# Start of a four-layer decoder trunk: order of the first loads, and the banks of the first norm's transposes

## The reference

```python
h = x
h = h + _even_mixer(_rmsnorm(h, norm_mix_even), ...)     # layer 0
...
def _rmsnorm(x, g):
    y = x * rsqrt(mean(x * x, axis=-1) + 1e-6)
    return y * g

def _even_mixer(h, ...):
    proj = h @ w_in                                       # 256 x 1024 @ 1024 x 2560
    qa, ka, va, ub, vb = split(proj, [512, 1024, 1536, 2048])
    qa, ka = rope(qa), rope(ka)                           # then differential attention
    lam = exp(sum(lam_q1 * lam_k1)) - exp(sum(lam_q2 * lam_k2)) + lam_init
    vb = layernorm(gelu(vb), sgu_ln_g, sgu_ln_b)
    ws = where(causal, sgu_w, 0)                          # 4 groups of 128 x 128
    mixed = einsum('gpq,bnqgc->bnpgc', ws, vb) + sgu_b
...
```

## Time and profile before

| | |
|---|---|
| median of 3 runs | 1367.97 us (1367.27 to 1369.31) |
| the profiled execution's own time | 1367.54 us |
| its span | 1365.8 us |
| TensorE matmul busy | 1344.9 us, 98% of the span |
| VectorE busy | 1129.7 us, 83% |
| ScalarE busy | 1006.0 us, 74% |
| granted TensorE clock, mean | 0.998 |

### The profile page before, as it was taken

The page is one execution under the profiler, slowest core; times in us unless marked ns, Lnnn a source line. Parts: engine busy times, 40 slices in busy tenths (PEclk is TensorE's granted clock), DMA queues, the critical chain, the costliest instruction groups (busy, mean ns, idle before and its releaser), DMA issues.

```text
span 1365.8 us, 19316 instructions
## 1 busy us (share of the span) xinstructions
PE 1344.9 (98%) x6874; PEld 1137.8 (83%) x6874; DVE 1129.7 (83%) x1153; ACT 1006.0 (74%) x1184; POOL 93.4 (7%) x117
## 2 busy tenths in 40 slices
PE   8999999999999999999999999999999999999997
PEld 7779989988788888888888888888888888888885
DVE  5675655566569999998999999999999999999996
ACT  6664544457558878788878888887888888788775
POOL 2201000000038600000000000000000000000010
PEclk9999999999999999999999999999999999999999
DMA  9457854354589999999999999999999999999960
GB/s 329 174 201 272 313 186 155 125 184 148 183 299 381 388 394 397 396 391 370 387 384 370 378 394 377 371 391 378 376 368 393 371 379 388 383 369 383 391 248 33
DMA packets 180621, 436.96 MB, mean 320 GB/s; under 512 B 4070, under 2 KB 8332, under 8 KB 180572
## 3 DMA queue, kind: packets, MB, share of 16 engines
q1 hardware_dynamic: 176816, 422.74, 83.7%
q0 software_dynamic: 3680, 13.54, 2.7%
q10 hardware_dynamic: 76, 0.02, 0.0%
HBM read 423.18 MB, written 13.11 MB: 319 GB/s over the span
## 4 chain that ended last, share of the span: by engine, by line
PE 94%; DVE 2%; ACT 2%; issue 1%; DMA 0%; ACTq 0%; SPq 0%; DVEq 0%
PE ps L1615 27%; PE ps L1617 26%; PE ps L1616 26%; PE ps L1870 3%; PE ps L1871 3%; PE ps L1872 3%; PE ps L2148 2%; ACT w_hi L660 1%; DVE w_lo L1062 1%; PE ps L1673 1%; PE ps L1642 0%; PE ps L2116 0%; ACT e L715 0%; PE ps L1625 0%; DMA h<-in_x 0%
## 5 line engine op out<-in xcount | busy, mean ns | idle before, releaser
L1491 DVE TENSOR_TENSOR w_lo<-ring_a,w_hi 128x1024 fp32r<-128x1024 f32 x384 | 459.1, 1223 | 36.7 <-ACT w_hi L939 18.3
L939 ACT ACTIVATE w_hi<-ring_a 128x1024 fp32r<-128x1024 f32 x384 | 399.0, 1057 | 61.6 <-PE ps L1617 61.5
L1491 DVE TENSOR_TENSOR w_lo<-ring_b,w_hi 128x1024 fp32r<-128x1024 f32 x288 | 344.5, 1223 | 22.8 <-ACT w_hi L939 8.0
L1615 PE MATMUL ps<-w_hi,xg_hi 128*128 128x512 f32 x896 | 354.2, 395 | 0.1
L1617 PE MATMUL ps<-w_hi,xg_lo 128*128 128x512 f32 x896 | 349.2, 390 | 0.0
L1616 PE MATMUL ps<-w_lo,xg_hi 128*128 128x512 f32 x896 | 348.7, 389 | 0.0
L939 ACT ACTIVATE w_hi<-ring_b 128x1024 fp32r<-128x1024 f32 x288 | 300.7, 1059 | 50.3 <-PE ps L1617 50.3
L1062 DVE TENSOR_TENSOR w_lo<-ring_a,w_hi 128x1024 fp32r<-128x1024 f32 (+2 forms) x119 | 141.5, 1199 | 107.7 <-ACT w_hi L660 107.6
L660 ACT ACTIVATE w_hi<-ring_a 128x1024 fp32r<-128x1024 f32 (+2 forms) x119 | 121.7, 1032 | 125.7 <-PE ps L1872 63.7
L1615 PEld LDWEIGHTS ps<-w_hi,xg_hi 128*128 128x128 f32 x896 | 168.3, 188 | 35.9 <-DVE w_lo L1491 3.1
L1617 PEld LDWEIGHTS ps<-w_hi,xg_lo 128*128 128x128 f32 x896 | 168.1, 188 | 35.8
(11 more groups left out here) (333 smaller groups left out, 1388.1 us busy)
## 6 DMA issues: line engine op xcount, KB each, us to landing
ring_a<-in_moe_wg SPq DMA_DIRECT2D x40, 2048.0 KB, 10.3
ring_a<-in_moe_wu SPq DMA_DIRECT2D x32, 2048.0 KB, 10.4
ring_b<-in_moe_wd SPq DMA_DIRECT2D x32, 2048.0 KB, 9.7
ring_b<-in_moe_wu SPq DMA_DIRECT2D x24, 2048.0 KB, 10.7
ring_a<-in_moe_wd SPq DMA_DIRECT2D x24, 2048.0 KB, 9.9
ring_b<-in_moe_wg SPq DMA_DIRECT2D x16, 2048.0 KB, 11.0
ring_a<-in_ffn_wg SPq DMA_DIRECT2D x5, 2048.0 KB, 8.8
ring_a<-in_ffn_wu SPq DMA_DIRECT2D x5, 2048.0 KB, 8.0
```

Of the source, the lines that this page charges most:

```text
L939: nc.scalar.activation(w_hi[:, (Q1 + q) % NQ, 0:1024], slot(j % RING2)[:, 1024 * k:1024 * k + 1024], ACT.Copy).then_inc(hi_done, 1)
L1491: v.tensor_tensor(w_lo[:, (Q1 + q) % NQ, 0:1024], slot(j % RING2)[:, 1024 * k:1024 * k + 1024], w_hi[:, (Q1 + q) % NQ, 0:1024].bitcast(F32 ...
L1615: pe.matmul(out_, a_hi, w_hi[:, q, c0:c1], start=first, stop=False)
```

## The change

The first quantum of q is loaded ahead of x. The tensor x comes in two column halves of 512 (both token tiles), with the second quantum between them, each half with its own semaphore (`x_in`, `x_rest`). Unit 1 (k) is issued ahead of the rest of the tables, and the small loads on GpSimd wait for unit 1 in place of unit 0. Groups 0 to 3 of the first norm are transposed into four different banks (6, 7, 2, 3), so that `bank_free` waits only from group 4 on; `keep_pace` writes to bank 4. ScalarE and VectorE take quantum 0 ahead of groups 0 and 1, and quantum 1 ahead of groups 2 and 3. The transposes of `sgu_w` stand behind k's third quantum, and their way out of PSUM behind quantum 10.

```diff
         def fbank(k):
 
+            if k < 4:
+                return (6, 7, 2, 3)[k]
             return k % 2 if fills["mix_odd"] <= k < fills["mix_odd"] + 4 else 6 + k % 2
@@
             sp.dma_start(table[:, 0:P], consts_d[:, 0:P]).then_inc(ident_in, 16)
-            for t in range(T):
-                sp.dma_start(h[:, t, :], A["x"][0].rearrange("(t p) d -> p t d", p=P)[:, t]).then_inc(x_in, 16)
+            x_rows = A["x"][0].rearrange("(t p) d -> p t d", p=P)
@@
             for k in range(lead.quanta):
                 sp.dma_start(slot(0)[:, k * lead.quantum:(k + 1) * lead.quantum].rearrange("p (c n) -> p c n", c=per),
                              lead.src[:, per * k:per * (k + 1)]).then_inc(
                                  first_in[k] if k < lead.quanta - 1 else loaded[0], 16)
-            sp.dma_start(table[:, P:CONSTS], consts_d[:, P:CONSTS]).then_inc(const_in, 16)
+                if k < 2:
+                    sp.dma_start(h[:, :, 512 * k:512 * k + 512], x_rows[:, :, 512 * k:512 * k + 512]).then_inc(
+                        (x_in, x_rest)[k], 16)
@@
                              unit.src).then_inc(loaded[u % RING1], 16)
+                if u == 1:
+                    sp.dma_start(table[:, P:CONSTS], consts_d[:, P:CONSTS]).then_inc(const_in, 16)
@@ GpSimd
-            pool.wait_ge(loaded[0], 16)
+            pool.wait_ge(loaded[1], 16)
@@ ScalarE
-            for f in range(4):
-                head("mix_even", f, xt_hi, g="norm_mix_even")
-                hi_upto(f + 1)
-            act.wait_ge(x_in, 16 * T)
+            for half in range(2):
+                hi_upto(half + 1)
+                for f in range(2 * half, 2 * half + 2):
+                    head("mix_even", f, xt_hi, g="norm_mix_even")
+            hi_upto(4)
+            act.wait_ge(x_in, 16)
+            act.wait_ge(x_rest, 16)
@@
-            hi_upto(end("k") + 2)
+            hi_upto(end("k") + 3)
             k = fills["sgu_w"]
             evac(k, sgu_wT[:, :, :], ps[:, 6 + k % 2, :].rearrange("p (g q) -> p g q", g=4))
-            hi_upto(end("k") + 3)
@@ VectorE
-            for f in range(4):
-                rest("mix_even", f, (xt_hi, xt_lo), g="norm_mix_even")
-                lo_upto(f + 1)
+            for half in range(2):
+                lo_upto(half + 1)
+                for f in range(2 * half, 2 * half + 2):
+                    rest("mix_even", f, (xt_hi, xt_lo), g="norm_mix_even")
+            lo_upto(4)
@@ TensorE
             def bank_free(k):
-                if k >= 2:
+                if k >= 4:
                     pe.wait_ge(*emptied(k - 2))
@@
-            keep_pace(8, 3, P)
-            pe.wait_ge(x_in, 16 * T)
-            for f in range(4):
+            keep_pace(8, 4, P)
+            pe.wait_ge(x_in, 16)
+            for f in range(2):
                 turn("mix_even", f, h_chunk)
-                if f == 1:
-                    keep_pace(4, 3, P)
-                elif f == 2:
-                    keep_pace(3, 3, P)
+            keep_pace(4, 4, P)
+            pe.wait_ge(x_rest, 16)
+            for f in range(2, 4):
+                turn("mix_even", f, h_chunk)
+            keep_pace(4, 4, P)
@@
-                if kq == 0:
+                if kq == 2:
                     k = fills["sgu_w"]
```

More of the change, by code:

```diff
@@ L312, in slot @@
             return ring_a[:, s] if s < RING1 else ring_b[:, s - RING1]
-        ident_in, const_in, x_in, lead_gain_in, grow_in, gain_in, even_in, bands_in, odd_in, rw_in = map(sem, (
-            "ident_in", "const_in", "x_in", "lead_gain_in", "grow_in", "gain_in", "even_in", "bands_in", "odd_in", "rw_in"))
+        ident_in, const_in, x_in, x_rest, lead_gain_in, grow_in, gain_in, even_in, bands_in, odd_in, rw_in = map(sem, (
+            "ident_in", "const_in", "x_in", "x_rest", "lead_gain_in", "grow_in", "gain_in", "even_in", "bands_in", "odd_in",
+            "rw_in"))
         loaded = [sem(f"loaded{s}") for s in range(RING2)]
```

## The result

| | before | after |
|---|---|---|
| median of 22 runs each | 1368.03 us (1366.64 to 1369.95) | 1370.43 us (1368.26 to 1373.82) |
| ratio of the two, 95% interval | | 1.002 (1.0014 to 1.0025) |
| the profiled execution's own time | 1367.54 us | 1368.26 us |
| its span | 1365.8 us | 1366.5 us |
| start of the first projection matmul | 12.03 us | 11.34 us |

The kernel is slower by 2.4 us. The profiled execution shows less than that, because it is the fastest of its kernel: 1.66 us are lost up to the last matmul, and from its start to the end of the span it took 8.9 us where the other profiles of all kernels took 9.2 to 10.1.

A forecast was written before the change was run, and what follows sets the result against it. TensorE's matmuls bound the kernel; VectorE's quantum split ahead of group 1, with its bank wait, delayed the first projection matmul. Start -0.6 and new wait +0.7 gave +0.1 us: 1368.1 us on the median, range 1366.4 to 1370.2.

The forecast's parts named there:

- The start: First projection matmul: groups 2 and 3 wait only for x's second half, so it starts at 11.4 us, gaining 0.6.
- The small loads: GpSimd starts them at 17.8 us, done at 30.1; VectorE's lambda products wait, costing TensorE 0.7 us before quantum 7.
- everything from 35 us on within 0.2 us of where it was: Expected profile of all engines behind the start: no shift above 0.2 us from 35 us on.
- A: Small loads land later still, delaying quantum 7: a chain of 14.3 us gives net +2.1, 1370.1 us; chance 12%.
- B: Start gains, small loads cost nothing: 0.6 to 0.9 us faster, 1367.2, at most 2.4 us; chance 10%.
- C: x lands late; if its second half lands past 10.2 us, net about 0.7 us slower, 1368.7; chance 6%.
- The 3, 92 and 5%: Whole kernel's time: chances of faster by more than 0.2%, within 0.2%, and slower by more than 0.2%.

The follow-up runs named there:

- 929: ScalarE instruction count of the kernel before (1368.03 us) and of changed kernels with one wait less on ScalarE; the changed kernel with only that edit: 1368.55 us, 1.001.
- 930: ScalarE instruction count of the changed kernel (1370.43 us), its variants without a wait removed, and the kernel before with one wait more (1370.35 us, 1.0021).
- 934: Changed kernel with eight more already met waits on ScalarE, packed into four instructions: 1370.05 us, 1.0021 to before.
- the repeat: The changed kernel run once more, unedited: 1370.78 us, 1.0028 to before.
- the version with both late: Changed kernel with VectorE's lambda products and the transposes of `sgu_w` moved later, ScalarE one wait less; run twice: 1368.23 us (1.0002) and 1366.75 us (0.9993) to before.

## Why the prediction was wrong

- **The start: right in its order of events, and lucky in its last digit.** Groups 2 and 3 at 9.60 (9.65 forecast), ScalarE's quantum 4 at 17.70 (17.8), the first projection matmul at 11.34 (11.4). The gain of 0.6 was 0.69 between these two profiles. Over all profiles the first projection matmul stands at 11.50, 12.03 and 12.30 with the old start and at 11.20 to 12.77 with the new one (9 of 11 by 11.68), so a single pair could have shown much more or nothing.
- **The small loads: right, and a little dearer.** GpSimd began at 17.98, the mask started at 30.41 and the lambda products at 30.37 (30.1), a chain of 12.4 us. Quantum 7 came at 32.38 (32.3). From 32.38 TensorE took 5.63 us to the first transposes of q at 38.01, where before it took 5.49: the first matmul after the idle stretch alone takes 0.34 to the next start in place of 0.23. So the net of the start was +0.3 at 38 us, not +0.1, and it was still +0.26 at 1346 us.
- **The failed step: "everything from 35 us on within 0.2 us of where it was".** True up to 1346 us but for a tenth, and false behind. The change splits one wait of ScalarE in two, and the prediction has no term for it: it was put at nothing without a reason. The wait cost nothing where it stands (the start went as reckoned), but one instruction more shifts all the code behind it, and the stall at the last loop moved with the count of instructions. The reading that fits its place at 929, 930 and 934 is that the loop's end crossed the border of a code block. The wait for that block was there before as well, 0.85 us behind the loop, with the loop's turns beside it. Now it is 2.05 us ahead of them: 2.02 more between the two instructions (2.05 against 0.03), 0.81 less behind the loop (0.85 against 0.04), and 0.20 more in the turns (1349.94 to 1351.49 against 1347.67 to 1349.02). That gives 1.4, all of it on TensorE's path.
- **The size.** 0.3 and 1.4 give 1.7 us, 1369.7 on the median. The rest of the 2.4 us is, in part, what the profile of the repeat shows: an idle stretch of 2.1 us on TensorE was followed by half the clock in 2 of the 7 profiles with 930 or 934 instructions (1.6 us each) and in none of the 7 with 929. In the timed runs, 17 of 84 with 930 or 934 lie above 1371.5 us, 1 of the 57 of the edited kernels with 929, and none of the 118 of before. What the 17 are is open: the two executions seen at half the clock took 1370.28 and 1370.05 us, below that mark, so half the clock alone doesn't put a run above it; with the slow pace on top it would. Timed runs leave no trace.
- **The rivals.** A had the right sign and the wrong place: the small loads took 12.4 us, not 14.3 or 15. B and C did not happen. None of the three looked past 60 us, and the range had no case for the engines' code. The 3, 92 and 5% were drawn over the start alone.

The Trainium skill has a rule that would have pointed there (Runtime: NRT & Kernel Launch, "Instruction fetch mechanics"): code is fetched in blocks of 256 instructions, and a taken branch to a target outside the two blocks at hand makes the engine wait for a fetch. The stall of 2.45 us ahead of the target at 934 agrees with it as far as a wait at the jump goes; how many blocks were at hand, no run shows. At 929 and 930 the target itself ran 0.43 us after the jump, and the engine stopped one or two instructions further on; the page doesn't describe that case, and the traces show it (0.85 us behind the loop, 2.05 and 2.01 us inside it). The code's place in memory was not read; that the border lies between the last two instructions of the loop at 930 is concluded from where the engine stands.

What stays open: why the kernel before with one more wait lost 2.7 us in the median where its profile shows 1.4 of it; the reordered transposes of groups 0 to 3 in four banks were not tried apart from the order of the loads; and whether the version with both late gains its 0.6 us. Its faster heap (16 of 23 runs) lies about 1366.7, that of before about 1367.3, which would be that gain, but the heaps were split after the fact and the intervals hold 1.

## What to carry to other kernels

Count the instructions that an edit adds to each engine's program, waits included, wherever the program has jumps behind the edit, and read the stretch behind each jump on the path in both traces: here one wait that was already met cost 2.7 us in the median. When work at the start changes and the end moves, do not look for a long chain between them first; compare idle time put down to "issue" line by line at the end. And when a load is made later, look at every engine that waits for it, not only at the one whose work was moved out of the way.

## What the runs showed of the hardware

- A met wait at 11.8 us moved a stall of 2.0 us at 1347 us ahead of three turns of a loop (between its last two instructions), and so onto the path: ratio 1.0021.
- Two paces of the same matmuls under a granted clock of 1.00, 113.3 and 117.8 ns, in two executions of one program, between 127 and 181 us.
- The start wanders as well. The eight transposes of x took 1.97 us, against 1.10 in the profile before, in the second profile of the kernel with both late, as in that of the copy of before, and the first projection matmul came at 12.77 there against 11.43; the granted clock stands at 1.00 from 0 to 11 us in both. TensorE's timelines, the first profile, then the second:

```profile
7.01 1.56 PE L1634 MATMUL ps<-table,h 128*128 128x128 f32 x8 [0.39 <-DMA h<-in_x]
...
9.68 1.09 PE L1634 MATMUL ps<-table,h 128*128 128x128 f32 x8 [0.21 <-DMA h<-in_x]
```

```profile
7.40 1.97 PE L1634 MATMUL ps<-table,h 128*128 128x128 f32 x8 [0.68 <-DMA h<-in_x]
...
10.87 1.25 PE L1634 MATMUL ps<-table,h 128*128 128x128 f32 x8
```

One profile of each kernel is thus no measure of a start to better than a microsecond: the first matmul of the program before stood at 12.03, 12.30 and, with one wait more, 11.50.
